# Causal masks of a sparse-attention block: added by TensorE into the scores' accumulation instead of by VectorE in PSUM

## The reference

```
s = einsum(q, k) * scale                 # q, k normalised per head, 512 x 512 for each head and branch
p = masked_softmax(s, key_pos <= t)      # causal: keys after the query are left out
o = einsum(p, v)                         # o = g0 * o_cmp + g1 * o_sel + g2 * o_win
```

## Time and profile before

| what | value |
|---|---|
| median of 3 runs | 3155.65 us (3155.05 to 3157.06) |
| the profiled execution, its own time | 3155.81 us |
| its span | 3154.0 us |
| mean granted clock of TensorE | 0.958 |
| busy: TensorE, weight loads, VectorE, ScalarE, GpSimd | 93%, 73%, 50%, 30%, 6% |
| the chain that ended last, by engine | TensorE 80%, VectorE 13%, ScalarE 4% |

### The profile page before, as it was taken

One profiled execution on the slowest core, in us unless ns is written; L12 is line 12 of the kernel. 1 busy time (PEld: TensorE's weight loads), 2 busy tenths in 40 slices (PEclk: granted clock), 3 DMA queues, 4 the chain that ended last, 5 costly groups with the idle time before them and its releaser, 6 DMA issues.

```text
span 3154.0 us, 38209 instructions
## 1 busy us (share of the span) xinstructions
PE 2933.1 (93%) x15996; PEld 2302.0 (73%) x15996; DVE 1569.0 (50%) x2466; ACT 952.8 (30%) x1441; POOL 203.9 (6%) x136
## 2 busy tenths in 40 slices
PE   7999998999999989989889999778897899989999
PEld 5775786888888867766668888544565588778887
DVE  3464435433233354257555554489976733343333
ACT  2154533222122132145333232310124522232222
POOL 2000000200000002000010000054410000000000
PEclk9999998999999999999999999888877999999999
DMA  6231000232332212100013232111120033223332
GB/s 245 87 110 58 25 27 28 74 115 100 127 112 109 79 49 74 59 29 1 14 61 100 87 116 84 47 58 42 46 81 32 11 97 97 90 74 94 100 95 85
DMA packets 67770, 238.20 MB, mean 76 GB/s; under 512 B 7440, under 2 KB 10640, under 8 KB 66960
## 3 DMA queue, kind: packets, MB, share of 16 engines
q1 hardware_dynamic: 67312, 234.20, 22.7%
q10 hardware_dynamic: 288, 1.57, 0.1%
HBM read 233.64 MB, written 2.10 MB: 75 GB/s over the span
## 4 chain that ended last, share of the span: by engine, by line
PE 80%; DVE 13%; ACT 4%; issue 3%; DMA 1%; POOL 0%; SPq 0%; DVEq 0%; ACTq 0%; POOLq 0%
PE PSA L562 78%; PE PSA L754 1%; ACT Y L1387 1%; DVE Y L1933 1%; DVE WS L1761 1%; DVE stat L1915 1%; DVE Y L2238 1%; DVE Y L1932 1%; DVE Y L2235 1%; DVE Y L2234 1%; DMA Y<-in_early 1%; DVE Y L1834 1%; DVE stat L2319 1%; ACT Y L1634 0%; ACT WS L1304 0%
## 5 line engine op out<-in xcount | busy, mean ns | idle before, releaser
L562 PE MATMUL PSA<-HS,WS 128*128 128x512 f32 (+1 forms) x7104 | 1494.5, 372 | 61.5 <-DVE HS L1781 44.5
L562 PEld LDWEIGHTS PSA<-HS,WS 128*128 128x128 f32 x7104 | 1241.4, 191 | 326.9 <-issue 81.4
L1761 DVE TENSOR_TENSOR WS<-W,WS 128x1024 fp32r<-128x1024 f32 (+2 forms) x358 | 407.7, 1140 | 714.4 <-ACT WS L1304 713.5
L1304 ACT ACTIVATE WS<-W 128x1024 fp32r<-128x1024 f32 (+2 forms) x358 | 351.3, 983 | 1039.2 <-PE PSA L562 688.7
L562 PE MATMUL PSA<-YS,WS 128*128 128x512 f32 (+1 forms) x2688 | 562.1, 370 | 3.5 <-DVE YS L2351 3.5
L562 PEld LDWEIGHTS PSA<-YS,WS 128*128 128x128 f32 x2688 | 470.4, 189 | 93.0 <-DVE YS L2351 3.9
L562 PE MATMUL PSA<-Y 128*64 128x128 f32 (+9 forms) x2240 | 348.4, 365 | 64.7 <-DVE Y L2248 39.4
L562 PEld LDWEIGHTS PSA<-Y 128*64 128x64 f32 (+4 forms) x2240 | 202.0, 166 | 171.7 <-issue 91.5
L1287 ACT ACTIVATE Y<-PSA 128x512 f32<-128x512 f32 (+3 forms) x89 | 63.4, 713 | 328.7 <-PE PSA L562 325.3
L1680 POOL TENSOR_SCALAR X<-X 128x768 f32<-128x768 f32 (+1 forms) x32 | 64.5, 2045 | 1373.7 <-DVE HS L1781 1373.7
L562 PE MATMUL PSA<-Y,C 128*128 128x512 f32 (+2 forms) x220 | 102.4, 600 | 22.9 <-ACT Y L1619 7.8
(11 more groups left out here) (250 smaller groups left out, 2228.4 us busy)
## 6 DMA issues: line engine op xcount, KB each, us to landing
W<-in_weights SPq DMA_DIRECT2D x396, 512.0 KB, 3.6
Y<-in_early SPq DMA_DIRECT2D x4, 2048.0 KB, 19.6
W<-in_weights SPq DMA_DIRECT2D x24, 256.0 KB, 2.9
X<-in_x SPq DMA_DIRECT2D x4, 768.0 KB, 20.9
W<-in_weights SPq DMA_DIRECT2D x24, 128.0 KB, 2.4
Y<-in_ssm ACTq DMA_DIRECT2D x1, 1024.0 KB, 6.5
out<-X SPq DMA_DIRECT2D x1, 1024.0 KB, 4.8
C<-in_consts SPq DMA_DIRECT2D x1, 948.5 KB, 31.9
```

Of the source, the lines that this page charges most:

```text
L562: return pe.matmul(out, lhsT, rhs, start=first, stop=last)
L1304: act.activation(WS[:, n % R_RING, 0, 0:f], W[:, c % W_RING, 0:f], ACT.Copy)\
L1761: tt(WS[:, n % R_RING, 1, 0:f], W[:, c % W_RING, 0:f], WS[:, n % R_RING, 0, 0:f].bitcast(F32), ALU.subtract).then_inc(weights_split, 1)
```

## The change

In `nsa_scores` the score products of a unit are split. First come the products of the last 128 columns (from `at` on) of both heads, left open. Then two products with the identity as weights and `after` as the moving operand are accumulated onto them, one for each head. Last come the products of the columns before `at`, for units with i > 0. The semaphore goes on the last product. VectorE's addition of `after` in PSUM goes, and its maximum follows the wait for the scores directly.

```
--- before.py
+++ after.py
@@ -1204,10 +1204,17 @@
                 take(key, n % 2)
                 if turn(key) > 1:
                     pe.wait_ge(psum_drained[slot(key)], turn(key) - 1)
+                at = nsa_width(u) - P
                 for t in range(2):
                     r = slice(HD * t, HD * t + HD)
-                    ins = mm(PS[slot(key)][:, t * S:t * S + nsa_width(u)], QN[r, p, i * P:(i + 1) * P],
-                             (KSL, KWN)[b][r, p // 2, 0:nsa_width(u)], True, True)
+                    mm(PS[slot(key)][:, t * S + at:t * S + at + P], QN[r, p, i * P:(i + 1) * P],
+                       (KSL, KWN)[b][r, p // 2, at:at + P], True, False)
+                for t in range(2):
+                    ins = mm(PS[slot(key)][:, t * S + at:t * S + at + P], const("ident"), const("after"), False, True)
+                for t in range(2 if at else 0):
+                    r = slice(HD * t, HD * t + HD)
+                    ins = mm(PS[slot(key)][:, t * S:t * S + at], QN[r, p, i * P:(i + 1) * P],
+                             (KSL, KWN)[b][r, p // 2, 0:at], True, True)
                 ins.then_inc(psum_filled[slot(key)], 1)
 
             def nsa_turn(u, n):
@@ -2314,8 +2321,6 @@
                     key, w = (u, "scores"), nsa_width(u)
                     dve.wait_ge(psum_filled[slot(key)], turn(key))
                     both = PS[slot(key)].rearrange("p (t c) -> p t c", t=2)
-                    diagonal = both[:, :, w - P:w]
-                    link(tt(diagonal, diagonal, const("after").unsqueeze(1).broadcast_to((P, 2, P)), ALU.add))
                     dve.tensor_reduce(nsa_stat(n)[0], both[:, :, 0:w], AX_X, ALU.max, negate=True)\
                         .then_inc(row_max, one("row_max", u))
                 if 1 <= n <= len(NSA_UNITS):
```

## The result

| | before | after |
|---|---|---|
| median | 3157.06 us (3155.05 to 3158.0, 5 runs) | 3168.99 us (3167.2 to 3172.19, 5 runs) |
| the profiled execution, its span | 3155.81, 3154.0 us | 3170.51, 3168.7 us |
| from the first maximum of the stretch to the first dense product behind it | 96.87 us | 110.08 us |

The changed kernel is slower, ratio 1.0041 with a 95% interval of 1.0026 to 1.0056. Forecast were 3164.3 us, which is 8.6 over 3155.65; measured are 3168.99, which is 11.9 over the median of the kernel before beside it, and 13.2 us more in the stretch of the two profiled executions.

What follows compares the result with a forecast made beforehand. Waits, with no engine full, were taken to bound the stretch. The first round's +3.5 us and three others' 3 x 1.7 = 5.1 made +8.6: 3155.65 + 8.6 = 3164.3 us, 8-in-10 range 3155.5 to 3170.

Steps and rivals of the forecast that it cites:

- The bound and what is removed: Stretch bound by waits; 32 VectorE mask adds go, 20 of them worth 9.2 us at most.
- the chain: Sequence of waits between engines that sets the stretch's length; 20 of 32 mask adds lie on it, 0.46 us each.
- the first round: First eight units, starting at half clock with full clock from 2420: +3.9, less about 0.4 for earlier clock, +3.5 us.
- The products: Two f32 identity products added per unit on TensorE, 0.22 us each, 0.44 for two.
- The change of shape: TensorE switching array shape inside a unit: 0.17 us each, two more for i > 0, 0.34.
- The sum for a round: Later round of eight units, TensorE's work and waits together: 24.65 us, +1.7 a round.
- The four steps: Round of eight units (head pair, query block i, branch) taken two units at a time: 6.3, 5.2, 5.9, 7.25 us.
- the walk: Adding TensorE's ordered work and waits from scores to scores, two units a step; old terms gave 23.2 us a round.
- Waits: Per round: transposes' wait for ScalarE's copy from 8.5 to about 3 to 4 us, VectorE's for scores 3.6 to over 8.
- The first (free changes inside a unit, 3156): Rival: shape changes inside a unit are free, a unit pays 0.44 for 0.46, +0.3 us, 3156; chance 0.18.
- The second (products that hide): Rival: identity products stream like transposes (0.21) and shape changes are free, -5.3 us, 3150.3; chance 0.07.
- The third (more for each product and change): Rival: weight loads stay open, 0.6 us for the products and 0.3 a shape change, +20 us, 3175; chance 0.10.

Runs made afterwards that it cites:

- e1: Kernel before without VectorE's mask add and without identity products, scores left unmasked; median 3150.26 us, ratio to the kernel before 0.9969.
- e2: Changed kernel with VectorE's add put back for the identity products, so only the score products are split; 3159.79 us, ratio to the kernel before 1.0002.
- e5: Changed kernel with each identity product cut into two of 64 rows, array shape staying 64x128; 3159.55 us, ratio to the kernel before 1.0000.
- e9: Changed kernel, same order and all 128 rows, with identity and mask in bf16; 3159.88 us, ratio to the kernel before 1.0000.
- e10: Changed kernel measured once more, unaltered; 3169.14 us, ratio to the kernel before 1.0038.
- e8: Changed kernel with 58 dense products, results unread, filling TensorE's idle time ahead of the stretch; 3164.57 us, ratio to the kernel before 1.0021.
- e7: Kernel before with 58 dense products, results unread, filling TensorE's idle time ahead of the stretch; 3156.39 us, ratio to the kernel before 0.9995.
- e4: Changed kernel with VectorE's add kept as well, so the mask is added twice; 3172.18 us, ratio to the kernel before 1.0048.
- e3: Changed kernel with score products whole and first, the identity products behind them next to the transposes; 3164.29 us, ratio to the kernel before 1.0006.
- e6: Changed kernel with whole score products first, then identity and mask in bf16 as four products of 64 rows; 3152.58 us, ratio to the kernel before 0.9978.

## Why the prediction was right in its direction and short in its size

**The bound and what is removed** stood. e1 gained 8.2 us in the stretch where the adds on the chain had been put at 9.2 at most.

**Where the error lies.** The stretch grew by 13.2 us and not by 8.6: of the 4.6 us that are missing, 2.9 are in the first round (+6.4 for +3.5) and 1.7 in the three others (+6.8 for +5.1).

**The products** were sized right: 0.44 us for two, at 2442.54 to 2442.98, as taken from the earlier trace rows. The split is free (e2).

**The change of shape** was the right cause, as e5 (the changes gone, the columns kept) and e9 (most of the columns' time gone, the changes kept) show, but mis-sized: taken at 0.17, measured at 0.22 and 0.20 inside the unit. The row that said so was in the prediction, the rest of 0.20 behind the scores of 256 columns; the 0.17 was the idle time before the next load, not the whole price. A unit with i > 0 pays 0.86 and not 0.78. For the same reason the sign that was named, weight loads with an idle of about 0.17 before the identity group, did not show: the loads at 2442.54 and 2445.72 follow the end of those before by 0.13, and the price is seen only from start to start.

**The sum for a round.** Forecast 24.65, measured 25.09. The four steps were forecast at 6.3, 5.2, 5.9 and 7.25 and measured at 6.48 (2438.81 to 2445.29), 5.32, 5.98 and 7.31. With 0.20 for a change the walk gave every variant's later round to within 0.2 us, except e5 and e9, where it was 0.4 short and 0.45 over.

**The first round** is the term that failed: forecast +3.5, measured +6.4, and +5.3 in e10. The prediction had let the clock come back at about the same place, or earlier because TensorE is fuller, and had taken off 0.4 us for that; that the clock might move by microseconds it had named only as a sign of being wrong. It came back later: at 2431 after a start at 2410.57, where before it was 2420 after 2408.69. And the round that is TensorE's own pays for the clock, while the one bound by waits hardly does.

The changed kernel's first round took 20.41, 26.38 and 27.43 us with 0, 15.8 and 18.1 us at half clock (e8, e10, and the profile after), so each microsecond at half clock cost it 0.38. The kernel before took 20.94 and 21.06 with 6.7 and 9.7 (e7, and the profile before), 0.04 for each. At 0.38, the 9.7 us of half clock of the kernel before would make the changed kernel's first round 24.1 us, +3.0 (an estimate from these rows), so that the rest of the 6.4, some 3 us, goes with the later return of the clock. These slopes rest on three executions of the changed kernel and two of the one before, and no profile of the one before had over 9.7 us at half clock.

What sets the moment at which the clock comes back is left open: 15.6 to 18.1 us of the first round went by at half clock in both plain profiles of the changed kernel and in e4 and e9, but 5.5 and 2.3 in e3 and e5, whose TensorE is busy for 95% and 90% of that round (99% in the changed kernel, 96% in e4 and e9). So it is also open how much of the extra half clock belongs to the change and how much to the execution.

**Waits.** VectorE's wait for scores was forecast over 8 and is 9.2; the transposes' was forecast at 3 to 4 and is 1.9.

**The rivals.** The first (free changes inside a unit, 3156) falls with the loads of the changed kernel (0.22 and 0.20 inside a unit) and with e5, which gets 0.40 us a unit back. So the Trainium skill's rule of the drain between tiling modes (TensorEngine Tiling, Tiling Modes) holds here without a wait between the groups too, at 0.20 to 0.22 us each between f32 products. The early load of weights (the Trainium skill, TensorE: Matmul & The Clock Gate, Part 2) did not cover it here. Had it done so, the first rival would have come out and not the second, as the prediction has it: free changes alone give 3156, and the second wants faster products as well. The second (products that hide) needed a unit below 0.43 us; it was none for f32 products, but e6, which pays 0.12 and no change, is that case and is 0.22% faster. The third (more for each product and change) did not come.

**Medians.** In the twelve profiles the first maximum of the stretch starts between 2404.79 and 2416.11, though e7 and e8 alone have more products ahead of it, and the kernel before spread from 3152.33 to 3164.15 over 27 executions. So two single spans, or two medians of few, are not a measure of this change. I trust the ratio of 1.004 since it came twice, and the parts of the stretch.

## What to carry to other kernels

In this kernel moving work from VectorE onto TensorE paid only where the added products kept the array's shape and took little time as well: the right shape alone (e5) and few columns' time alone (e9) both ended level with the kernel before, and only e6, with both, was faster. The same mask cost 0.86 us a unit as f32 identity products of 128 rows between products of 64 rows, and 0.12 in bf16 on the same 64 rows. Put a product of another shape next to work that already has it, as e3 did for 1.5 us a round. And before giving a wait-bound loop more TensorE work, look at the granted clock there: here up to 9.7 us at half the clock were nearly free while waits bound the loop, and they were not once TensorE bound it.

## What was not expected of the hardware

The granted clock stayed at 0.50 for 19.4 us in which TensorE was busy all the time by the profile (19.43 of 19.43 us), while a stretch with gaps in the kernel before got it back after 11 us. Busy time in the profile did not tell when the clock would rise. Nor did it tell when it would fall: in e7 TensorE was busy without a gap from 2402 to 2414, and the clock was at 0.50 from 2404 to 2410, while TensorE ran through the last of 64 instructions of 64x16 and the first of the 22 filling products:

```profile
2404.00:2410.00 6.00, 6.00 (x32) 5.29 (x31) 4.86 (x13) 0.25 (x1) 0.00 (x0) 0.50 0.79 250
```

And the price of a change of shape was not the same out of two f32 products (0.20) as out of two bf16 products (0.11, e9).
